# The triangular mask and the zero keys' scores of one attention, written into the score bank by TensorE instead of VectorE

## The reference

```
in_window = jnp.abs(k_off[None, :] - q_off[:, None]) <= WINDOW      # k_off: -128 to 255, WINDOW = 128
start = b * Q_BLOCK                                                # block b of 128 queries
kb = lax.dynamic_slice_in_dim(k_pad, start, span, axis=1)           # keys padded by 128 zeros on either side
kpos = start - WINDOW + k_off
valid = in_window & ((kpos >= 0) & (kpos < N))[None, :]
s_win = jnp.where(valid, jnp.einsum('bqhgd,bkhd->bhgqk', qblk, kb), NEG_BIG)
s_ctx = jnp.einsum('bqhgd,bkhd->bhgqk', qblk, k_c)
p = softmax_with_sink(jnp.concatenate([s_win, s_ctx], axis=-1))
return einsum(p[..., :span], vb) + einsum(p[..., span:], v_c)
```

## Time and profile before

| | before |
|---|---|
| runs, us | 3530.07, 3517.62, 3531.79 |
| median, us | 3530.07 |
| profiled execution, us | 3522.28 |
| its span, us | 3519.8 |
| TensorE busy | 3437.2 us, 98% |
| VectorE busy | 2139.8 us, 61% |
| ScalarE busy | 1405.8 us, 40% |
| mean granted TensorE clock | 0.995 |

### The profile page before, as it was taken

How to read it: one execution, slowest core, us unless ns; L and a number is a source line. 1 busy time by engine, 2 the same in 40 slices (tenths; PEclk the granted TensorE clock), 3 DMA queues, 4 the chain that set the end, 5 groups by cost and what they waited for, 6 DMA issues and landing times.

```text
span 3519.8 us, 58526 instructions
## 1 busy us (share of the span) xinstructions
PE 3437.2 (98%) x25712; PEld 2909.3 (83%) x25712; DVE 2139.8 (61%) x3256; ACT 1405.8 (40%) x2252; POOL 171.2 (5%) x306
## 2 busy tenths in 40 slices
PE   9999999999999999999979999999999999999998
PEld 7878886899888888778859997768887888779998
DVE  5765455787667635675575554553558854566775
ACT  4213434665422333232455543452343333345553
POOL 0110000000011001111000000110001100010000
PEclk9999999999999999999999999999999999999999
DMA  6664121000356524666434541222236533334453
GB/s 255 229 203 150 49 85 39 3 4 10 109 185 203 179 84 169 226 204 128 127 128 158 183 139 60 72 61 72 96 106 197 189 143 107 100 98 136 170 186 114
DMA packets 122382, 453.68 MB, mean 129 GB/s; under 512 B 10416, under 2 KB 18736, under 8 KB 95120
## 3 DMA queue, kind: packets, MB, share of 16 engines
q1 hardware_dynamic: 88368, 332.60, 27.3%
q0 software_dynamic: 33760, 117.34, 11.1%
HBM read 447.24 MB, written 1.94 MB: 128 GB/s over the span
## 4 chain that ended last, share of the span: by engine, by line
PE 85%; DVE 8%; ACT 3%; DMA 2%; issue 1%; SPq 0%; DVEq 0%; ACTq 0%
PE bank L1262 84%; DVE WR L2202 2%; ACT W L1818 2%; DMA ring<-in_w_ada 2%; DVE W L2211 2%; PE bank L1548 1%; ACT WR L1818 1%; DVE W L2202 1%; DVE small L2542 1%; DMA ring<-in_odd_w_in 0%; DVE X L2211 0%; DVE HL L2202 0%; DVE W L2206 0%; ACT H L1818 0%; DVE H L2202 0%
## 5 line engine op out<-in xcount | busy, mean ns | idle before, releaser
L1262 PE MATMUL bank<-HH,WR 128*128 128x512 f32 (+1 forms) x9312 | 2407.1, 345 | 18.1 <-DVE HL L2202 10.1
L1262 PEld LDWEIGHTS bank<-HH,WR 128*128 128x128 f32 x9312 | 1624.6, 190 | 257.7 <-issue 24.7
L1262 PE MATMUL bank<-HL,WR 128*128 128x512 f32 (+1 forms) x4656 | 1589.8, 341 | 0.0
L1262 PEld LDWEIGHTS bank<-HL,WR 128*128 128x128 f32 x4656 | 884.3, 190 | 96.4
L2202 DVE TENSOR_TENSOR WR<-ring,WR 128x2048 fp32r<-128x2048 f32 (+3 forms) x300 | 673.4, 2249 | 470.7 <-ACT WR L1818 470.1
L1818 ACT ACTIVATE WR<-ring 128x2048 fp32r<-128x2048 f32 (+3 forms) x300 | 561.7, 1879 | 685.6 <-PE bank L1262 604.2
L1818 ACT ACTIVATE W<-bank 64x256 f32<-64x256 f32 (+4 forms) x586 | 273.0, 474 | 655.3 <-PE bank L1262 618.8
L2211 DVE SCALAR_TENSOR_TENSOR W<-ring,vec,W 128x1024 f32<-128x1024 f32 x308 | 381.9, 1279 | 77.3 <-DMA ring<-in_w_mod 54.0
L1262 PE MATMUL bank<-W 64*64 64x64 f32 (+5 forms) x4030 | 277.3, 263 | 21.4 <-ACT W L1818 19.5
L1262 PEld LDWEIGHTS bank<-W 64*64 64x64 f32 (+3 forms) x4030 | 195.7, 143 | 82.2 <-issue 39.3
L1818 ACT ACTIVATE W<-bank,small 128x512 f32<-128x512 f32 (+2 forms) x183 | 113.4, 622 | 204.5 <-DVE small L2542 149.2
(11 more groups left out here) (123 smaller groups left out, 2349.6 us busy)
## 6 DMA issues: line engine op xcount, KB each, us to landing
ring<-in_ffn_in SPq DMA_DIRECT2D x88, 1024.0 KB, 5.6
ring<-in_w_mod POOLq DMA_DIRECT2D x128, 512.0 KB, 4.3
ring<-in_w_in SPq DMA_DIRECT2D x52, 1024.0 KB, 5.1
ring<-in_ffn_out SPq DMA_DIRECT2D x44, 1024.0 KB, 4.8
ring<-in_w_up SPq DMA_DIRECT2D x44, 1024.0 KB, 4.9
ring<-in_w_ada POOLq DMA_DIRECT2D x80, 512.0 KB, 4.2
ring<-in_w_down SPq DMA_DIRECT2D x22, 1024.0 KB, 4.9
W<-in_m SPq DMA_DIRECT2D x4, 2048.0 KB, 15.9
```

The costliest lines, as they stand in the source:

```text
L1262: return e.matmul(o, l, r, start=start, stop=stop, skip_group_check=True)
```

## The change

The units of query block 0 carry `mask` in place of `bias`, and `scores` on TensorE does the work: after the score matmul of a `mask` unit it multiplies the identity by `wmask` into columns 128 to 255, accumulating onto the scores, and the semaphore that VectorE waits on is raised by this matmul. Before the score matmul of a `fill` unit it multiplies the identity by `wmask` into columns 0 to 127. VectorE's copy and its `own()` are gone for the `fill` units; for the `mask` units no `bias` is there any more, so its addition and `own()` are not issued (other attentions still use `bias`). There are 16 units of each kind.

```diff
@@ odd_mixer
                 if qt == 0:
-                    u["bias"] = (C("wmask"), P)
+                    u["mask"] = C("wmask")
                     u["lo"] = P
                 else:
                     u["fill"] = C("wmask")
@@ scores, on TensorE
                         o = take(("S", name, j, m))
-                        mm(o[:, c:c + kl.shape[1]], ql, kl, True, True).then_inc(MM.sem, MM.mark(("S", name, j, m)))
+                        u = a["units"][j]
+                        if "fill" in u:
+                            mm(o[:, 0:P], C("ident"), u["fill"], True, True)
+                        x = mm(o[:, c:c + kl.shape[1]], ql, kl, True, "mask" not in u)
+                        if "mask" in u:
+                            x = mm(o[:, c:c + P], C("ident"), u["mask"], False, True)
+                        x.then_inc(MM.sem, MM.mark(("S", name, j, m)))
                         shut(("S", name, j, m))
@@ att, on VectorE
-                        if "fill" in u:
-                            copy(bank[:, 0:P], u["fill"])
-                            own()
```

## The result

| | before | changed kernel |
|---|---|---|
| median of 20 runs each, us | 3523.56 | 3534.44 |
| lowest to highest, us | 3517.13 to 3531.85 | 3526.14 to 3540.72 |
| ratio | | 1.0031 [1.0024, 1.0038] |
| profiled execution, its span, us | 3522.28, 3519.8 | 3531.9, 3529.9 |
| first scores to last outputs of the attention, us | 98.42 | 106.01 |

The changed kernel is 0.31% slower, 10.9 us by the medians. That is inside the half per cent that I had called "same", but the sign is not the forecast's, and it is more than all 7.7 us of TensorE work that I had counted as added. (The before kernel's median is 3523.56 over 20 runs, where three had given 3530.07.)

The account below looks back on a forecast made before the run. TensorE bounds the run (busy 98%), but within the attention the bound passes from TensorE to VectorE, DMA, then VectorE and ScalarE. +1.7 - 1.7 + 0 - 1.0 = -1.0 us, giving 3521.3 or 3529.1; forecast 3527, range 3515 to 3536.

Parts of the forecast that it names:

- same: Whole run: time within about 0.5% (17.6 us) of before, chance 0.92, against faster 0.03 and slower 0.05.
- A: 1751 to 1769 us, first scores to units 6 and 7: TensorE without a gap, seven identity matmuls add 1.7 us.
- B: 1769 to 1787 us, to the outputs at 1787.57: VectorE bound, six removed instructions give 1.95 us, 0.25 given back, -1.7.
- C: 1787 to 1810 us: two DMA slab loads bound, identity matmuls hidden under TensorE's wait for a slab, 0.
- D: 1810 to 1843 us: VectorE and ScalarE bound, eight removed instructions, TensorE late next at unit 22, -1.0 us.
- the outer bound of the relief: VectorE's 16 additions and 16 copies removed, 0.33 and 0.32 us each: at most 10.4 us gained.
- Rival 2: Attention: TensorE is the bound, its gaps too small for the identity matmuls, +7.7 us at most, 3537.8; chance 0.15.
- rival 1: Attention: VectorE's relief comes through and the lower clock goes away, about -5 us, 3525; chance 0.14.
- rival 3: Lower clock stays after a longer wait in C, 1 to 2 us a stretch, 3548 or more; chance 0.04.
- rival 4: Mask matmul or fill unseen or too early, a wait or work stays: 3530 or up to 7.7 us above; chance 0.05.

Follow-up runs that it names:

- the two kernels with TensorE's part alone: Before kernel, VectorE's additions and copies kept, plus the 32 identity matmuls: in the changed kernel's order 1.0033, with a pair's identities together 1.0008.
- the first experiment: Changed kernel with the identity matmuls of a pair of units kept together, ahead of or behind both score matmuls: 0.9995 to before, 3518.97 us against 3519.68.
- the repeat: The changed kernel run again with nothing altered: 1.0028 to before, 3529.94 us against 3519.43, attention 109.2 us.

## Why the prediction was right or wrong

**What failed is the price of the added matmuls**, in the words of the prediction "the trace has exactly these already, as fillers", "32 x 0.24 = 7.7 us of TensorE, the outer bound of a loss". The fillers have the same shape, but stand behind a pair, never inside one. I priced the instructions and not the place. The added cost on TensorE is 23.4 us, of which some 16 us is the lost overlap. A mask pair with its identities takes 2.34 us to the next matmul in the changed kernel and 1.32 us (1748.16 to 1749.48) with the identities behind the pair; 16 x 1.02 = 16.3 us. The busy times of the two kernels with TensorE's part alone differ by 16.4 us, those of the changed kernel and the first experiment by 19.2. What is left is near the 7.7 us of the forecast, so the price of 0.24 us holds for identities beside a pair, not inside one. It was to be seen: the earlier trace rows has four score instructions of 384 columns in 0.92 us, 0.60 ns a column, where the fillers of the earlier trace rows need 0.92 ns a column (0.235 us for two instructions of 128), and the order listing of the change shows the identity matmuls inside each pair, which I quoted without asking what ran beside what. The outer bound that I called one was none.

The four parts can be measured between the same instructions of each trace: the first scores, those of units 6 and 7, the outputs behind the nine fillers, the scores of units 18 and 19, the last outputs. Before, these start at 1751.45, 1768.38, 1787.57, 1809.62 and 1849.87 us, in the changed kernel at 1753.60, 1774.92, 1795.44, 1816.20 and 1859.61, with the identities of a pair together at 1748.16, 1766.61, 1783.81, 1805.46 and 1844.20. Against before, in us:

| | A | B | C | D |
|---|---|---|---|---|
| forecast | +1.7 | -1.7 | 0 | -1.0 |
| changed kernel | +4.4 | +1.3 | -1.3 | +3.2 |
| identities of a pair together | +1.5 | -2.0 | -0.4 | -1.5 |

**A: +1.7 us** came out as +4.4. The scores of units 6 and 7 start 21.3 us after the first ones (1753.60 to 1774.92), not 16.9; from pair to pair the delay grows by 1.7, 0.8 and 1.9 us. I had said that I would be wrong if an identity matmul took more than 0.27 us; from start to next start it takes 0.32 us ahead of a pair (1758.90 to 1759.22) and 0.42 inside one (1754.44 to 1754.86), before the lost overlap.

**B: -1.7 us** did not happen; it was +1.3. VectorE was to be the bound until 1787 us. It was busy 9.60 of the 20 us from 1765 to 1785, and the 1.95 us that it was to save there brought nothing forward. Over the attention it has 21.3 us of waits for TensorE ahead of its row maxima (14.3 us before, ahead of the additions and copies).

**C: 0** came out as -1.3. TensorE's added work went under the waits for slabs, of which 1.3 us remained out of 4.7, so the cover was nearly used up; and the two loads on the chain were shorter, 7.13 and 6.35 us in place of 7.66 and 6.68.

**D: -1.0 us** came out as +3.2 (+6.4 in the repeat, with more of it at half clock). The mechanism was right, "what is late next is TensorE", but the size was off: TensorE waits only 2.5 us for ScalarE in the whole attention (11.4 us before), so it was late nearly everywhere, not just at unit 22.

**The other terms were sound where the overlap is kept.** With the identities of a pair together, that is with the cost structure that I had assumed, the table's last row has each part within half a microsecond of its forecast. It is one profile on either side, and the time, -0.7 us by the medians, 0.9995 [0.9986, 1.0004], agrees with the sum of -1.0 without testing it, since the interval is some 3 us wide on either side. And the outer bound of the relief, 10.4 us, against about 6 us measured with mask and fill left out: the chain's 14 instructions had said 4.5.

**The rivals.** Rival 2, TensorE as the bound, is what happened in kind, at 0.15. The rule of the Trainium skill ("Perfetto Trace Analysis", Identifying the Most-Contended Engine), to optimize the engine of the highest occupancy first, pointed the right way, though with the identities of a pair together the same added load cost nothing measurable. But the mechanism that I gave rival 2 was capped by the same 7.7 us. Its time, 3537.8 against the first median, comes near the measured 3534.44 only because that median was high: against 3523.56 it would have been 3531.3. Rivals 1, 3 and 4 fell. The granted clock still falls to 0.50 within the attention: for about 6.8 us in the profile before, in two stretches of which the earlier trace rows shows one, for 3.4 us in the changed kernel (1839 to 1842 us) and 10.2 us in its repeat. So no gain from the clock can be told, as rival 1 had it, nor a loss that explains the result, as rival 3 had it.

**The range and the centre.** 3515 to 3536 held the median 3534.44 by 1.6 us, and by luck: I had taken the centre at 3527 from a median of three that was 6.5 us above that of twenty. The chance of "same" by half a per cent, 0.92, came true; the sign and the size of the change within it did not.

## What to carry to other kernels

Before putting an instruction between two matmuls on half of the array's rows, look whether they run side by side: less time for each column of data than other matmuls of the trace need (here 0.60 ns a column for a pair, 0.92 for the fillers, 1.18 for one score matmul alone, two instructions of 384 columns in 0.91 us). Keep such neighbours together and place anything of another shape ahead of or behind them. And a cheap instruction's price from elsewhere in the trace is a price for that place only; an order listing shows what it would come between.

## What the runs showed of the hardware

- Two fp32 matmuls of 64 rows by 128 columns on different rows, with 384 columns of data each, take 0.92 us together, and 0.91 us each when a matmul of another shape stands between them, even one of 0.15 us.
- A matmul on the free rows runs beside them if its weights are 64 x 128 (it started 0.01 us later), and does not if they are 64 x 32 (it started 0.84 us later).
- An fp32 identity matmul of 128 columns takes 0.235 us among its like, 0.24 us behind a score pair (two in 0.47), 0.27 to 0.32 us ahead of one, and 0.42 us between two score matmuls. With rounded operands it is one instruction, and two of them have 0.44 us where four had 0.71.
- The relief of VectorE was worth 2.6 to 4.6 us with the identities of a pair together. In the changed kernel's order none could be told, within some 4 us.
